# A mixture-of-experts layer in fp32: 64-column matmuls issued as pairs of 32-column matmuls in the first of two layers

## The chip, the cores and the metric

The kernel runs on one NeuronCore of one Trainium2 chip. The metric is the device time of one execution in microseconds (us), from its start to its end; lower is better. All arithmetic is fp32. TensorE's matrix multiply takes a stationary operand (here the token columns, loaded with LDWEIGHTS) and streams a moving operand (here the expert's weight rows) past it, up to 512 columns at a time, into PSUM. The number of stationary columns is the number of PSUM partitions that are written, and the partition at which the output starts says which columns of the array are used.

## What is computed

The program is two transformer blocks one behind the other, each of two layers. What matters here is the second block's feed-forward part, an expert-choice mixture of 16 experts. Layer 0 runs it on two token sets (512 latent tokens and 256 context tokens), layer 1 on the latent tokens only.

```python
def ec_moe(h, w_router, w_gate, w_up, w_down):
    bsz, n_tok, d = h.shape                       # d = 1024
    cap = EC_CAPACITY * n_tok // N_EXPERTS        # 64 of 512 latent tokens, 32 of 256 context tokens
    aff = jax.nn.softmax(jnp.einsum('bnd,de->bne', h, w_router).astype(jnp.float32), axis=-1)
    g, idx = lax.top_k(jnp.swapaxes(aff, 1, 2), cap)
    xs = jax.vmap(lambda hb, ib: hb[ib])(h, idx)
    hid = jax.nn.silu(jnp.einsum('becd,edf->becf', xs, w_gate)) * jnp.einsum('becd,edf->becf', xs, w_up)
    ye = jnp.einsum('becf,efd->becd', hid, w_down) * g[..., None].astype(h.dtype)
    return jax.vmap(lambda yb, ib: jnp.zeros((n_tok, d), h.dtype).at[ib.reshape(-1)].add(yb.reshape(-1, d)))(ye, idx)
```

Each expert has three weight matrices of 1024x1024 fp32 (4 MB each).

## The kernel before, in words

The program runs the first block, then for each layer of the second block a mixer (attention and convolution), a router, and the 16 experts (`pe_experts`, `experts_act`, `experts_dve`, `experts_pool`, one function per engine). Each engine's instructions stand in program order; engines meet through semaphores. The experts run as 8 rounds of two (`rounds`): the first round is written out, the other seven are a hardware loop.

**TensorE** does for each expert: the gate product, the up product, the turning (transposes) of the next expert's gathered rows (`turn_xs`, L1042), the transposes of the hidden rows (L1095, L1100), and the down product. Each product (`product`, L1048 to L1064) goes through 8 steps, one for each 128 rows of the weight matrix (`for k in range(KD)`), so an expert has 24 steps. A step waits for its weight slot (a 128x1024 piece, 512 KB), and then issues:

- two matmuls for the 64 latent tokens (L1055), one for each half of the 1024 weight columns. The stationary operand is 64 columns wide, the moving operand 512. Half 0 writes partitions 0 to 63 and half 1 partitions 64 to 127 of the same PSUM bank, `dst`.
- in layer 0 also four matmuls for the 32 context tokens (L1060), one for each quarter of the weight columns: 32 stationary columns, 256 moving ones, into partitions 0, 32, 64 and 96 of another bank, `dstc`.

The profile counts each fp32 matmul as two MATMUL and two LDWEIGHTS records, so a step of layer 0 has 4 and 8 of each, and one of layer 1 has 4.

**The weights** come through 24 slots (`expert_slot`: 12 of a ring, and 12 in buffers that are free by then, which the profile names mixT, mixcT, v, probs, qz and kz). SyncE issues the load of a slot for the next expert (L2369) as soon as the step that used it has signalled `moe_k`. So the loads run one expert ahead of the matmuls.

**GpSimd** gathers the token rows of a later expert (L1231; 96 rows of 4 KB in layer 0, 64 in layer 1) and adds the finished rows to the output in DRAM (L1272). **ScalarE and VectorE** apply the activation, copy products out of PSUM and scale the results.

After layer 0's experts the residual and norm of that layer run, then layer 1's mixer, router and experts.

Of the kernel before, what the change touches and what calls it, by code (L numbers as in the profile page):

```python
# [27 lines left out]
KD = D // P  # L28
# [21 lines left out]
CAP = 2 * SEQ // EXPERTS  # L50
# [80 lines left out]
def build_program(nc, a, known, banks, sem_names):  # L131
# [6 lines left out]
    with ExitStack() as ctx:  # L138
# [3 lines left out]
        def sem(name):  # L142
            if name not in sems:
                sems[name] = ctx.enter_context(nc.semaphore(name))
            return sems[name]

        def done(name, event=None, by=1):

            if not frozen[0]:
                counts[name] = counts.get(name, 0) + by  # L150
                marks[(name, event)] = counts[name]
            return sem(name), by

        def at(name, event=None):

            return sem(name), known.get((name, event), 1)

        def emptied(job):

            for name in ("evac_act", "evac_dve"):  # L160
                if (name, job) in known:
                    return at(name, job)
            return at("evac_act", job)
# [85 lines left out]
        ps = ctx.enter_context(nc.psum_tensor("ps", [P, 8, 512], F32))  # L249
# [744 lines left out]
        def at_round(name, event, i, back=0):  # L994

            per = known.get(("per_round", event[0], name), 1)
            return sem(name), i * per + max(known.get((name, event), 1) - back * per, -back * per + 1)
# [8 lines left out]
        def expert_slot(s):  # L1006
            return ring[:, s, :] if s < RING else spare[s - RING]

        def slot_count(s, l, u, i):

            return i * 32 + (banks.get(("moe_slot", l, s), 0) + 16 * (u + 1))

        def rounds(eng, l, body):

            before = dict(counts)
            body(0)
            per = {k: counts[k] - before.get(k, 0) for k in counts if counts[k] != before.get(k, 0)}
            frozen[0] = True
            with eng.Fori(1, ROUNDS) as i:
                body(i)  # L1020
            frozen[0] = False
            for k, n in per.items():
                marks[("per_round", l, k)] = n
                counts[k] = before.get(k, 0) + ROUNDS * n

        def settled(eng, count):


            return count if first_round(count) else eng.compute_val(count)

        def first_round(i):
            return isinstance(i, int)

        def pe_experts(pe, l):
            rows = CAP + (CAP_C if l == 0 else 0)
            G, U, GC, UC, Y, YC = 2, 3, 4, 5, 6, 7

            def turn_xs(i, u, event):

                for hb in range(2):  # L1040
                    for c in range(4):
                        mm = nc.tensor.transpose(ps[:, hb, c * 96:c * 96 + rows],  # L1042
                                                 xs[0:rows, (u + 1) % 2, (4 * hb + c) * P:(4 * hb + c + 1) * P],
                                                 ident[0:rows, 0:rows])
                    mm.then_inc(*done("xs_turned", (l, event, hb)))

            def product(i, u, m, lhs, dst, dstc, last_event):


                for k in range(KD):  # L1050
                    s = KD * m + k
                    pe.wait_ge(sem(f"slot{s}"), slot_count(s, l, u, i))
                    w = expert_slot(s)
                    for half in range(2):
                        mm = nc.tensor.matmul(ps[64 * half:64 * half + 64, dst, :], lhs[:, k, 0:CAP],  # L1055
                                              w[:, half * 512:(half + 1) * 512], start=(k == 0), stop=(k == KD - 1),
                                              skip_group_check=True)
                    if l == 0:
                        for q in range(4):
                            mm = nc.tensor.matmul(ps[32 * q:32 * q + 32, dstc, 0:256], lhs[:, k, CAP:CAP + CAP_C],  # L1060
                                                  w[:, q * 256:(q + 1) * 256], start=(k == 0), stop=(k == KD - 1),
                                                  skip_group_check=True)
                    mm.then_inc(*done("moe_k", (l, u, m, k)))


            pe.wait_ge(*emptied(("topT", l)))
            pe.wait_ge(*emptied(("grow", l, 1, 1 if l == 0 else 0, 1)))
            pe.wait_ge(sem("gathered0"), known.get(("gather", l, 0), 16))
            turn_xs(0, -1, "first")

            def body(i):
                for u in range(2):
                    b = u

                    if u == 0:
                        if first_round(i):
                            pe.wait_ge(*at("xsT_act", (l, "first")))
                            pe.wait_ge(*at("xsT_dve", (l, "first")))
                        else:
                            pe.wait_ge(*at_round("xsT_act", (l, 1), i, 1))  # L1080
                            pe.wait_ge(*at_round("xsT_dve", (l, 1), i, 1))
                    else:
                        pe.wait_ge(*at_round("xsT_act", (l, 0), i))
                        pe.wait_ge(*at_round("xsT_dve", (l, 0), i))
                    product(i, u, 0, xsT[:, b, :, :], G, GC, None)
                    product(i, u, 1, xsT[:, b, :, :], U, UC, None)

                    count = settled(pe, gather_count(l, u, i))
                    pe.wait_ge(*emptied(("topT", l)))
                    pe.wait_ge(sem(f"gathered{(u + 1) % 2}"), count)  # L1090
                    turn_xs(i, u, u)

                    pe.wait_ge(*at_round("hid", (l, u, 0), i))
                    for c in range(4):
                        mm = nc.tensor.transpose(ps[:, G, c * P:(c + 1) * P], hid[:, c * P:(c + 1) * P], ident)  # L1095
                    mm.then_inc(*done("hid_turned", (l, u, 0)))
                    if l == 0:
                        pe.wait_ge(*at_round("hid", (l, u, 1), i))
                        for c in range(2):
                            mm = nc.tensor.transpose(ps[:, GC, c * P:(c + 1) * P], hidc[:, c * P:(c + 1) * P], ident)  # L1100
                        mm.then_inc(*done("hid_turned", (l, u, 1)))
                    pe.wait_ge(*at_round("hidT", (l, u), i))

                    if not (first_round(i) and u == 0):
                        pe.wait_ge(*at_round("ye_copied", (l, 1 - u), i, 1 - u))
                    product(i, u, 2, hidT, Y, YC, None)

            rounds(pe, l, body)

        def gather_count(l, u, i):  # L1110

            return i * 16 + (known.get(("gather", l, 1 - u), 16) + 16 * u)
# [1322 lines left out]
```

## Time and profile before

| | us |
|---|---|
| median of 3 runs | 3107.52 |
| lowest and highest run | 3103.11, 3107.66 |
| span of the profiled execution, first to last instruction | 3105.2 |
| TensorE busy in it | 2721.4 (88%) |
| VectorE, ScalarE, GpSimd busy | 1024.7, 745.5, 254.5 |

For the profiled execution the page gives its span and no separate total; the three runs are other executions. Layer 0's experts lie between about 1423 and 2076 us of the span, layer 1's between about 2558 and 3066 us. In the rows of the trace a busy matmul has the time until its last result is out, so the times of neighbouring matmuls overlap; how fast a stream of them runs is read from the starts.

### The profile page before, as it was taken

The page shows a single profiled execution, that of the slowest core. Times are in us where ns is not written, and L with a number is a line of the kernel's source. Part 1 is how long each engine was busy: PE and PEld are TensorE (multiplying, and loading weights), DVE is VectorE, ACT ScalarE, POOL GpSimd, SP SyncE. Part 2 cuts the span into 40 slices and gives each one's busy share as a digit, 9 for nine tenths or more (in the row PEclk, how much of TensorE's full clock was granted, in tenths as well). Part 3 has the DMA queues.
Part 4 walks back from the last instruction along what each step waited for, and adds up shares of the span by engine and source line. Part 5 has one row for each costly group of instructions (what it writes and reads, how often), then busy time and mean ns, then how long its engine had stood idle before and what let it go on. Part 6 is the DMA issues. An engine that isn't in the chain of part 4 may idle for free. (4 is left out here: it accounts for less than half of the span.)

```text
span 3105.2 us, 44305 instructions
## 1 busy us (share of the span) xinstructions
PE 2721.4 (88%) x17378; PEld 1465.2 (47%) x17378; DVE 1024.7 (33%) x2278; ACT 745.5 (24%) x1857; POOL 254.5 (8%) x314
## 2 busy tenths in 40 slices
PE   7998999999989899987999999976899969788783
PEld 3664684665867666782222222213666753222221
DVE  3123430224347763553111111126752551011012
ACT  2233411343221453331111111113243321000000
POOL 1000100001000010021000000010000021001001
PEclk9999999999999999987999999997899979999997
DMA  7342614444331011047999999971002059999996
GB/s 217 106 125 67 182 36 114 124 114 120 106 82 34 1 27 48 31 160 278 334 327 330 329 332 331 324 213 39 26 8 75 28 202 387 389 397 396 390 397 233
DMA packets 354638, 579.26 MB, mean 187 GB/s; under 512 B 18592, under 2 KB 242048, under 8 KB 354496
## 3 DMA queue, kind: packets, MB, share of 16 engines
q1 hardware_dynamic: 339040, 523.47, 49.0%
q0 software_dynamic: 15312, 53.67, 6.2%
q8 instruction: 100, 1.64, 0.2%
q14 instruction: 42, 0.34, 0.0%
q10 hardware_dynamic: 144, 0.14, 0.0%
HBM read 554.12 MB, written 23.07 MB: 186 GB/s over the span
## 5 line engine op out<-in xcount | busy, mean ns | idle before, releaser
L441 PE MATMUL ps<-hT,ring 128*128 128x512 f32 x1088 | 482.3, 603 | 5.7 <-ACT hT L1403 4.3
L1055 PE MATMUL ps<-ring,hT 128*64 128x512 f32 x1536 | 424.8, 647 | 63.1 <-DMA ring<-in_w_gate 29.7
L441 PEld LDWEIGHTS ps<-hT,ring 128*128 128x128 f32 x1088 | 209.4, 194 | 264.5 <-issue 257.1
L687 PE MATMUL ps<-ring,mixT 128*128 128x128 f32 x2048 | 232.6, 276 | 0.8 <-DVE mixT L1539 0.8
L1055 PEld LDWEIGHTS ps<-ring,hT 128*64 128x64 f32 x1536 | 86.3, 141 | 308.6 <-DMA ring<-in_w_gate 121.3
L687 PEld LDWEIGHTS ps<-ring,mixT 128*128 128x128 f32 x2048 | 231.0, 193 | 1.3 <-DVE mixT L1539 1.3
L1190 DVE TENSOR_TENSOR work<-work,ps 128x512 f32<-128x512 f32 x32 | 22.0, 688 | 632.3 <-PE ps L1060 326.3
L487 PE MATMUL ps<-kz,qz 96*128 96x256 f32 (+3 forms) x384 | 156.9, 492 | 26.3 <-DVE qz L1965 10.7
L1212 DVE SCALAR_TENSOR_TENSOR hcT<-hcT,gates,work 64x1024 f32<-64x1024 f32 (+1 forms) x48 | 61.3, 1276 | 354.5 <-ACT hcT L1156 221.3
L1126 ACT ACTIVATE hT<-ps,modc 128x64 f32<-128x64 f32 x204 | 62.3, 403 | 400.3 <-PE ps L1042 400.3
L1580 ACT ACTIVATE probsT<-ps 128x512 f32<-128x512 f32 (+3 forms) x280 | 120.3, 455 | 140.2 <-PE ps L527 113.3
L1567 ACT ACTIVATE probs<-ps,col 128x256 f32<-128x256 f32 (+5 forms) x216 | 136.5, 632 | 70.9 <-DVE col L1517 37.0
L513 PE MATMUL ps<-const,probs 128*128 128x128 f32 x752 | 122.9, 280 | 20.5 <-DVE probs L1531 18.4
L1055 PE MATMUL ps<-mixT,hT 128*64 128x512 f32 x512 | 133.4, 612 | 7.0 <-DMA mixT<-in_w_up 6.9
L1513 DVE TENSOR_REDUCE col<-ps 128x1 f32<-128x256 f32 (+4 forms) x136 | 78.9, 580 | 178.1 <-PE ps L487 175.3
L1060 PE MATMUL ps<-ring,hT 128*32 128x256 f32 x1536 | 123.5, 393 | 0.0
L1272 POOL DMA_INDIRECT y_moe<-hcT,idx_to x32 | 46.3, 1447 | 918.2 <-DVE hcT L1212 891.8
L1152 ACT ACTIVATE hcT<-ps 64x512 f32<-64x512 f32 x64 | 37.9, 593 | 338.1 <-PE ps L1060 201.2
L1531 DVE TENSOR_SCALAR probs<-probs,col 128x256 f32<-128x256 f32 (+5 forms) x216 | 112.0, 519 | 7.6
L513 PEld LDWEIGHTS ps<-const,probs 128*128 128x128 f32 x752 | 89.9, 143 | 42.2 <-DVE probs L1531 30.9
L452 PE MATMUL ps<-ring,hT 128*128 128x128 f32 x896 | 103.0, 277 | 4.5 <-ACT hcT L1403 4.5
L452 PEld LDWEIGHTS ps<-ring,hT 128*128 128x128 f32 x896 | 102.8, 194 | 7.7 <-ACT hcT L1403 4.8
(275 smaller groups left out, 3386.3 us busy)
## 6 DMA issues: line engine op xcount, KB each, us to landing
ring<-in_w_gate SPq DMA_DIRECT2D x256, 512.0 KB, 8.9
ring<-in_w_up SPq DMA_DIRECT2D x128, 512.0 KB, 8.7
mixT<-in_w_up SPq DMA_DIRECT2D x128, 512.0 KB, 7.6
ring<-in_w_mod SPq DMA_DIRECT2D x96, 512.0 KB, 5.2
ring<-in_w_in SPq DMA_DIRECT2D x82, 512.0 KB, 7.3
mixcT<-in_w_down SPq DMA_DIRECT2D x64, 512.0 KB, 8.7
qz<-in_w_down SPq DMA_DIRECT2D x64, 512.0 KB, 11.8
kz<-in_w_down SPq DMA_DIRECT2D x64, 512.0 KB, 12.9
```

The source lines that it names most:

```text
L441: mm = nc.tensor.matmul(ps[:, b, 0:n], w[:, k, :], rhs[:, k, 0:n], start=(k == 0), stop=(k == KD - 1))
L452: mm = nc.tensor.matmul(ps[:, b, t * P:(t + 1) * P], lhs[:, k, t * P:(t + 1) * P], w[:, k, :], start=(k == 0), stop=(k == KD - 1))
L487: mm = nc.tensor.matmul(S[:, o:o + rhs.shape[-1]], lhs, rhs, start=lhs is not ident, stop=True, skip_group_check=True)
L513: mm = nc.tensor.transpose(ps[:, 4 + n % 2, i * P:(i + 1) * P], p_sbuf(u)[:, j * P:(j + 1) * P], ident)
L687: mm = nc.tensor.matmul(ps[:, b, c * P:(c + 1) * P], lhs[:, k, tl * P:(tl + 1) * P], ws[c][:, k, :], start=(k == 0), stop=(k == KD - 1))
L1055: mm = nc.tensor.matmul(ps[64 * half:64 * half + 64, dst, :], lhs[:, k, 0:CAP], w[:, half * 512:(half + 1) * 512], start=(k == 0), stop=(k ...
L1060: mm = nc.tensor.matmul(ps[32 * q:32 * q + 32, dstc, 0:256], lhs[:, k, CAP:CAP + CAP_C], w[:, q * 256:(q + 1) * 256], start=(k == 0), stop ...
L1126: ins = nc.scalar.activation(xsT[:, (u + 1) % 2, c, o:o + n], ps[:, 0, c * 96 + o:c * 96 + o + n], ACT.Identity, bias=sh, scale=sc)
L1513: nc.vector.tensor_reduce(nmax(u), s_psum(u), AX, ALU.max, negate=True).then_inc(*done("nmax", u))
L1531: nc.vector.tensor_scalar(p, p, rinv(u), None, ALU.mult).then_inc(*done("probs_normed", u))
L1567: nc.scalar.activation(p_sbuf(u), s_psum(u), ACT.Exp, bias=nmax(u), accum_out=rsum(u)).then_inc(*done("probs", u))
L1580: nc.scalar.activation(probsT[:, n % 2, blocks[0]:blocks[-1] + 1, :], ps[:, 4 + m % 2, 0:len(blocks) * P].rearrange("p (b q) -> p b q", q= ...
```

## The change

In `product`, where the layer is 0, the loop over halves has an inner loop over groups of 32 token columns. Each matmul of 64 stationary columns becomes two of 32 with the same moving operand, which write partitions `64*half` and `64*half + 32` of the same bank. In layer 1 the step of the inner loop is 64, so that the same matmul as before is issued there. The matmuls of the context tokens, the waits and the signals stay as they are.

```diff
@@ -1051,10 +1051,13 @@
                     s = KD * m + k
                     pe.wait_ge(sem(f"slot{s}"), slot_count(s, l, u, i))
                     w = expert_slot(s)
+                    step = 32 if l == 0 else CAP
                     for half in range(2):
-                        mm = nc.tensor.matmul(ps[64 * half:64 * half + 64, dst, :], lhs[:, k, 0:CAP],
-                                              w[:, half * 512:(half + 1) * 512], start=(k == 0), stop=(k == KD - 1),
-                                              skip_group_check=True)
+                        for g in range(0, CAP, step):
+                            o = 64 * half + g
+                            mm = nc.tensor.matmul(ps[o:o + step, dst, :], lhs[:, k, g:g + step],
+                                                  w[:, half * 512:(half + 1) * 512], start=(k == 0),
+                                                  stop=(k == KD - 1), skip_group_check=True)
                     if l == 0:
                         for q in range(4):
                             mm = nc.tensor.matmul(ps[32 * q:32 * q + 32, dstc, 0:256], lhs[:, k, CAP:CAP + CAP_C],
```

On TensorE, at the start of layer 0's experts, the instructions stand so (the shapes are stationary columns x moving columns; a row is a run of matmuls of one line; - is before, + is the change, whose lines stand 3 further down):

```order
-L1055 MATMUL ps<-ring,hT 64x512 x2
-L1060 MATMUL ps<-ring,hT 32x256 x4
...
+L1058 MATMUL ps<-ring,hT 32x512 x4
+L1063 MATMUL ps<-ring,hT 32x256 x4
```

Each pair of rows is one step. The order of the steps and of everything between them is the same; only the first run of each step has four matmuls in the place of two.

## Rows read from the trace of the kernel before

**Rows 1.** Layer 0's L1060 matmuls: records, duration ns min/median/max, first and last start.

```profile
L1060 PE MATMUL ps<-ring,hT x1536: 379/403/636, 1425.0 to 2053.6; 128*32 128x256 f32 x192
L1060 PE MATMUL ps<-mixT,hT x512: 379/391/403, 1445.7 to 2059.9; 128*32 128x256 f32 x171
```

**Rows 2.** Stretches of layer 0's experts and layer 1's: busy, PEclk, DMA share, GB/s.

```profile
1466.31:2075.88 609.57, 594.58 (x4534) 147.81 (x4530) 97.18 (x210) 89.06 (x241) 41.87 (x60) 1.00 0.94 321
2832.00:2864.00 32.00, 25.81 (x104) 6.63 (x104) 3.66 (x7) 3.07 (x7) 2.74 (x4) 0.95 1.03 393
```

**Rows 3.** Timeline of TensorE, layer 0: start us, us, engine line op [idle before].

```profile
1500.53 1.08 PE L1055 MATMUL ps<-qz,work 128*64 128x512 f32 x4
1501.54 0.64 PE L1060 MATMUL ps<-qz,work 128*32 128x256 f32 x8
...
1506.84 1.08 PE L1055 MATMUL ps<-ring,hT 128*64 128x512 f32 x4
```

**Rows 4.** Timeline of TensorE, layer 0, between up and down product.

```profile
1450.98 0.88 PE L1042 MATMUL ps<-const,hT 96*128 96x96 f32 x8
...
1453.69 1.08 PE L1055 MATMUL ps<-mixcT,work 128*64 128x512 f32 x4 [0.90 <-DVE work L1202]
...
2062.95 1.08 PE L1055 MATMUL ps<-mixcT,work 128*64 128x512 f32 x4 [0.90 <-DVE work L1202]
```

**Rows 5.** Timeline, one step of layer 0 in short windows: the records' later passes apart.

```profile
1466.32 1.08 PE L1055 MATMUL ps<-ring,hT 128*64 128x512 f32 x4
...
1466.80 0.60 PE L1055 MATMUL ps<-ring,hT 128*64 128x512 f32 x2
...
1467.32 0.42 PE L1060 MATMUL ps<-ring,hT 128*32 128x256 f32 x4
...
1467.56 0.40 PE L1060 MATMUL ps<-ring,hT 128*32 128x256 f32 x4
```

**Rows 6.** Timeline of TensorE, layer 1, steps of one shape whose weights had landed.

```profile
2825.88 1.06 PE L1055 MATMUL ps<-v,work 128*64 128x512 f32 x4
2826.74 1.06 PE L1055 MATMUL ps<-probs,work 128*64 128x512 f32 x4
2827.60 1.91 PE L1055 MATMUL ps<-qz,work 128*64 128x512 f32 x8
```

**Rows 7.** Timeline of TensorE, projections of the second block: shapes change, 128 stationary columns stay.

```profile
944.68 7.31 PE L452 MATMUL ps<-ring,hT 128*128 128x128 f32 x64
951.82 3.74 PE L452 MATMUL ps<-ring,hcT 128*128 128x128 f32 x32
955.39 7.07 PE L441 MATMUL ps<-hcT,ring 128*128 128x256 f32 x32
962.30 7.31 PE L452 MATMUL ps<-ring,hcT 128*128 128x128 f32 x64
...
985.08 13.90 PE L441 MATMUL ps<-hT,ring 128*128 128x512 f32 x32
998.81 1.46 PE L441 MATMUL ps<-hcT,ring 128*128 128x256 f32 x6
```

**Rows 8.** Timeline of TensorE, the modulation product: 32 stationary columns at four places.

```profile
138.24 1.96 PE L596 MATMUL ps<-ring,cond 128*32 128x128 f32 x64
140.12 0.49 PE L487 MATMUL ps<-kz,qz 96*128 96x128 f32 x2
```

**Rows 9.** Waits in layer 0's experts: total us, times, longest.

```profile
POOL y_moe L1272 <- DVE hcT L1212: 491.6, 15, 49.4
DVE work L1190 <- PE ps L1060: 298.1, 15, 20.0
```

**Rows 10.** Timeline of TensorE, layer 1: first wait for weights, later starts of down products.

```profile
2619.49 1.08 PE L1055 MATMUL ps<-mixT,hT 128*64 128x512 f32 x4 [1.29 <-DMA mixT<-in_w_up]
...
2657.91 1.94 PE L1055 MATMUL ps<-mixcT,work 128*64 128x512 f32 x8 [0.79 <-DVE work L1197]
...
2890.53 1.94 PE L1055 MATMUL ps<-mixcT,work 128*64 128x512 f32 x8 [0.97 <-DVE work L1197]
```

**Rows 11.** Start of both expert stages: first product of layer 1, first reload of layer 0.

```profile
1426.19 12.62 SPq L2369 DMA_DIRECT2D ring<-in_w_gate  x8
...
2557.74 12.59 PE L1055 MATMUL ps<-ring,hT 128*64 128x512 f32 x48 [1.24 <-ACT hT L1126]
```

## The prediction

> **What bounds the kernel now.** I read first which stage the change touches. Its matmuls are those of layer 0's experts, 16 experts of 24 steps, 384 steps. The list of one line's instructions for L1060, which exists in layer 0 only, puts them between 1425 and 2076 us [rows 1]. Then I read what each engine does there. From 1466.31 to 2075.88 us, 15 experts, TensorE is busy for 594.58 of 609.57 us at a granted clock of 1.00, that is 2.4 GHz; the DMA engines move 321 GB/s [rows 2]. In the list of waits of this stretch no matmul waits for a weight load; the others wait for TensorE: VectorE's first instruction of an expert waits up to 20.0 us for it, and GpSimd's scatter is behind that chain [rows 9]. So this stage lasts as long as TensorE's stream of steps, and every nanosecond of a step counts 384 times until something else becomes the bound.
>
> A step takes (1506.84 - 1500.53) / 4 = 1.5775 us, of which the two 64-column matmuls take 1.01 and the four 32-column ones 0.57 [rows 3]. Between the up and the down product there are 2.71 us of transposes and of waiting for hidden rows [rows 4]. 24 x 1.5775 + 2.71 = 40.57; measured from down product to down product over 15 experts it is (2062.95 - 1453.69) / 15 = 40.62. The model of a period holds to 0.05 us.
>
> **Where the 1.5775 us of a step go.** The short windows divide a step into its four passes: the 64-column group starts at 1466.32, its second pass at 1466.80, the 32-column group at 1467.32, its second pass at 1467.56 [rows 5], and the next step 1.5775 behind the first, at 1467.90. That makes passes of 0.48, 0.52, 0.24 and 0.34 us. What a pass costs when nothing changes between passes is read elsewhere. In layer 1, whose steps have only the 64-column pair, steps with landed weights start 0.86 us apart, 0.43 a pass [rows 6]. In the projections, with 128 stationary columns throughout, 32 records of 512 moving columns take 13.73 us, 0.429 each, and 32 of 256 take 6.91 us, 0.216 each [rows 7]. Four such passes are 2 x 0.429 + 2 x 0.216 = 1.290 us. A step of layer 0 takes 0.2875 us more: about 0.05 in its first pass, 0.09 in its second, 0.02 in the third, and 0.11 in the fourth.
>
> What is special about these steps is that the width of the stationary operand alternates, 64, 32, 64, 32. At each change there are two charges: the last pass before it is longer (0.09 and 0.11), as if the array had to run empty, and the first pass behind it is longer by about the time of a weight load that is not hidden (0.05 for 64 columns, 0.02 for 32). Where the width stays, neither is there: not in layer 1 [rows 6], and not in the projections, where both the moving length (128, 256, 512) and the bank change with no charge at the border [rows 7]. TensorEngine Tiling (Array Packing) of the Trainium skill, Key Properties, says that a change of tiling mode drains TensorE, but gives no price.
>
> **The change, part by part.**
>
> *Removed:* the change of width within a step and between steps of one product. All eight matmuls of a step are now 32 columns wide. By the sum above a step falls from 1.5775 to 1.290 us: 0.2875 x 384 = **110.4 us**. Bounds for this term: below, that some 5 ns per pass are added, the fixed part in [rows 7]: a pass is 0.1116 us for 128 columns (7.14 / 64) and 0.429 for 512, so 0.83 ns a column and 5 ns over; if the four-place passes had that twice, 0.27 a step, 103 us. Above, the full removal without any fixed cost, 0.297 a step, 114 us. I take 0.2875, since rows 7 are streams with the same lengths of pass.
>
> *Added:* two matmuls a step, that is four MATMUL and four LDWEIGHTS records more, 768 matmuls in all. If they ran behind the others, each step would double. They don't have to: the 32-column group of today starts four matmuls together, since all four records begin before the window at 1467.56 and 0.24 us later the next four start, where one alone streams 0.216 [rows 5]. The modulation product is the nearest row for a long stream of them: 64 records of 32 columns at four places, 128 moving columns, in 1.96 us with the following work at 140.12, 1.88 behind the start [rows 8]. That is 16 passes of at most 0.1175, against 0.1116 in [rows 7] with no tiling at all; the rest is the drain at its end. So four at once cost nothing over one, and issuing 8 records with their 8 loads per pass of 0.11 us keeps up. After the change there are 8 + 8 records per 0.43 or 0.22 us, a slower pace. I cost the added ones at nothing; the cover is the stream of moving columns, and if it were gone they would cost the rivals' prices below.
>
> *At the borders:* the first load behind the transposes is of 32 columns and not 64, 0.03 us less for two borders an expert, under 1 us in all, left out. The first two or three steps of the stage run below full clock and gain a little less or more; also left out.
>
> *What is late next.* The period becomes 24 x 1.290 + 2.71 + 0.05 = 33.7 us. ScalarE and VectorE need about 6 us each of it (89.06 and 97.18 in 15 experts [rows 2]); GpSimd's scatter has a wait of some 30 us to give [rows 9]. The weight loads are the candidate. Layer 1 is bound by them: there the DMA engines are at 1.03 and 393 GB/s [rows 2], and its period is (2890.53 - 2657.91) / 7 = 33.2 us [rows 10]. An expert of layer 0 moves the same 24 x 0.524 MB = 12.58 MB of weights, and 96 rows of 4 KB gathered and scattered in the place of 64: 13.37 MB against 13.11. The floor is 33.2 x 13.37 / 13.11 = 33.9 us, 0.2 more than TensorE needs. That does not yet stall it, since the loads are nearly an expert ahead. Layer 1 gives the lag: its loads can restart at about 2559 [rows 11]; the load that first makes TensorE wait is the 39th after that, due 39 x 33.2 / 24 = 54 us later, 2613; it is used at 2619.49 [rows 10], so about 7 us are to be added. In layer 0 the reloads start at 1426.19 [rows 11]; those for 15 experts are there by 1426 + 15 x 33.9 + 7 = 1942. TensorE's last step starts at 1423 + 16 x 33.7 + 1 = 1963. So the loads stay ahead to the end, by 21 us. I cost the loads at nothing in the stage and 1 us behind it, where the loads for layer 1's mixer now overlap the last scatter.
>
> **The sum.** 3105.2 - 110.4 + 1 = 2995.8 us of span. The median of the runs is 2.3 above the profiled span, so 2998 us.
>
> **Rivals.**
>
> *The loads become the bound* (chance 0.12). The DMA share, and not the bytes, may be the true measure: 0.94 at a period of 40.62 us; if 1.03 is the most, the floor is 40.62 x 0.94 / 1.03 = 37.1 us. The reloads would then end at 1426 + 15 x 37.1 + 7 = 1989.5, 26 us after the last step wants its slot. The gain is 84, the time 3024. For it: the share is already high. Against: layer 1 moves 393 GB/s through the same kind of loads [rows 2]. It decides from a floor of (1963 - 7 - 1426) / 15 = 35.3 us.
>
> *One weight load per pass is exposed* (0.05). With 32 columns the price is what the first pass has too much, 0.240 - 0.216 = 0.024 us; four passes, 0.096; the step is 1.386, the gain 73.5, the time 3034. Against it: no such gap in [rows 6] or [rows 8]. TensorE: Matmul & The Clock Gate of the Trainium skill, Part 3, says that a weight load overlaps a running matmul only if it is for another group of rows. All loads here are for all 128 rows, so by that rule they would be exposed, and the time would be this rival's or the next one's; the trace disagrees, at 0.43 us a pass in layer 1 where that rule wants 0.48.
>
> *Every weight load is exposed* (0.04), the other side. There are now 16 loads a step. If each held up the stream by 0.024 us, the step would be 1.290 + 0.384 = 1.674 us, 0.097 more than now: 37 us slower, 3145. It decides from 0.2875 / 16 = 18 ns a load. The place would be the four 512-column matmuls, of which pairs read the same weights; no row has just that. Against: 64 loads in 1.88 us [rows 8] leave 5 ns apiece over the streaming.
>
> *The width is not the cause* (0.05). If the 0.2875 us came from going back and forth between two banks and two lengths within one step, it would stay: 3107. Rows 7 change both without a charge, but every 8 records or more, not every two.
>
> **How the numbers follow.** The forecast has what is left, 0.74, and its own range is 2990 to 3004 (103 to 114 us gained, some us for the last loads and the runs' scatter of 4.6). With the first rival 0.86 are covered; the range so is 2990 to 3030. A difference of 0.2% (6 us) is about what a measurement of this kernel can tell from none. Faster: 0.74 + 0.12 + 0.05 = 0.91. Same: 0.05. Slower: 0.04.
>
> **What would show it.** In the profile of the changed kernel: steps of layer 0 that start 1.29 us apart, with four records at the start of each pass (1.39: exposed loads; 1.58: the width wasn't it); 24 of them and an unchanged 2.7 us between products, periods of 33.7; no matmul of layer 0 waiting for a weight load, with a DMA rate near 390 GB/s; layer 1 unchanged at periods of 33.2 and everything from the end of layer 0's experts on about 110 us earlier. Waits for the loads late in the stage with steps of 1.29 would be the first rival; a time within 6 us of before, or above it, would show the forecast wrong.

## The result, and the profile after

The changed kernel takes 3003.31 us (median of 4 runs, 2999.04 to 3020.04) against 3107.01 (median of 4 runs), a ratio of 0.9678 with a 95% interval from 0.9652 to 0.9704. The forecast was 2998, with a range from 2990 to 3030. The profiled execution took 3002.31 us, its span is 3000.5.

The timeline of TensorE in the stretch that [rows 3] show, in the changed kernel:

```profile
1505.00 1.04 PE L1058 MATMUL ps<-ring,hT 128*32 128x512 f32 x8
1505.86 0.61 PE L1063 MATMUL ps<-ring,hT 128*32 128x256 f32 x8
1506.29 1.04 PE L1058 MATMUL ps<-ring,hT 128*32 128x512 f32 x8
1507.15 0.61 PE L1063 MATMUL ps<-ring,hT 128*32 128x256 f32 x8
1507.58 0.61 PE L1058 MATMUL ps<-ring,hT 128*32 128x512 f32 x4
```

A step starts every 1.29 us where it was 1.5775. The 512-column group has twice the records and takes 0.86 us where it took 1.01, and the 256-column group, whose instructions are unchanged, takes 0.43 where it took 0.57. The second number points most plainly at what the change removes: nothing was done to L1063, yet it is faster beside neighbours of its own width. That the width of the neighbours decides this is tested in experiment 4.

The busy times by stretch, as in [rows 2] (busy of PE, PEld, DVE, ACT and POOL, then clock, DMA share, GB/s):

```profile
1600.00:1700.00 100.00, 97.03 (x1182) 40.46 (x1178) 19.43 (x42) 17.75 (x48) 8.36 (x12) 1.00 1.03 387
1800.00:1900.00 100.00, 97.03 (x1182) 40.53 (x1178) 19.43 (x42) 17.75 (x48) 8.35 (x12) 1.00 1.03 392
```

The DMA engines now run at the share and nearly the rate that they have in layer 1, and TensorE is still busy for 97% of the time. The list of waits of TensorE and its load queue in this stage names VectorE's hidden rows, and no weights. It also has a line that was not there before (who waited on whom: total us, times, longest):

```profile
PE ps L1058 <- DVE work L1205: 13.4, 15, 0.9
...
PE ps L1058 <- issue: 5.4, 1, 5.4
```

"issue" is a wait for nothing that the profile shows. The timeline has its place, between the fourth and the fifth expert:

```profile
1560.65 0.61 PE L1063 MATMUL ps<-kz,work 128*32 128x256 f32 x8
1566.67 1.94 PE L1058 MATMUL ps<-ring,hT 128*32 128x512 f32 x8 [5.41 <-issue]
1568.37 1.09 PE L1063 MATMUL ps<-ring,hT 128*32 128x256 f32 x8
1569.23 1.94 PE L1058 MATMUL ps<-ring,hT 128*32 128x512 f32 x8
1570.93 0.67 PE L1063 MATMUL ps<-ring,hT 128*32 128x256 f32 x8
```

This is the first jump back of TensorE's loop over rounds. Behind the pause one whole step runs with starts 2.56 us apart, twice the usual, at a granted clock of 0.50 in the window from 1565 to 1570 us: after the standstill the array is at its lower level, 1.2 GHz. That expert's period is 41.62 us; the other 14 are 33.75 to 33.85.

The starts of the down product give the account of the stage; they answer to [rows 4]:

```profile
1446.05 0.62 PE L1063 MATMUL ps<-mixT,hT 128*32 128x256 f32 x8
1446.60 0.88 PE L1042 MATMUL ps<-const,hT 96*128 96x96 f32 x8
...
1449.30 1.07 PE L1058 MATMUL ps<-mixcT,work 128*32 128x512 f32 x8 [0.90 <-DVE work L1205]
...
1964.60 1.07 PE L1058 MATMUL ps<-mixcT,work 128*32 128x512 f32 x8 [0.90 <-DVE work L1205]
```

From the first down product to the last it is 515.30 us where it was 609.26. The two ends of the stage are its first step and the first transpose of the next stage (L644). Before:

```profile
1423.14 1.98 PE L1055 MATMUL ps<-ring,hT 128*64 128x512 f32 x4 [2.12 <-ACT hT L1126]
...
2098.78 1.54 PE L644 MATMUL ps<-const,kz 128*128 128x128 f32 x6 [23.14 <-DVE kz L1304]
```

After:

```profile
1424.04 1.93 PE L1058 MATMUL ps<-ring,hT 128*32 128x512 f32 x8 [2.12 <-ACT hT L1129]
...
1998.33 1.97 PE L644 MATMUL ps<-const,kz 128*128 128x128 f32 x8 [23.20 <-DVE kz L1307]
```

So the stage lasts 574.3 us where it lasted 675.6, 101.4 less: 5.3 are gained up to the first down product, 94.0 between the first and the last, and 2.1 behind the last. The spans differ by 104.7. The rest lies in stretches whose instructions the change leaves alone: the stage starts 0.9 us later, and from L644 to the end of the span it is 1002.2 us where it was 1006.4. In the profiles of the experiments the stretch from L644 on takes between 1003.3 and 1006.2, and the stage starts between 1422.1 and 1427.9, so differences of some us there say nothing about the change.

### The profile page after: what moved, and what is told of

Read it like the earlier page. It is cut to its first block and busy times, and to the rows that moved or that the text cites. A ratio compares the mean times of both kernels' runs of the same rounds, so it can differ in the third digit from the quotient of the medians.

```text
span 3000.5 us, 47377 instructions
## 1 busy us (share of the span) xinstructions
PE 2611.7 (87%) x18914; PEld 1525.0 (51%) x18914; DVE 1022.8 (34%) x2278; ACT 744.5 (25%) x1857; POOL 255.1 (9%) x314
## 5 line engine op out<-in xcount | busy, mean ns | idle before, releaser
L1058 PE MATMUL ps<-ring,hT 128*32 128x512 f32 (+1 forms) x2304 | 417.9, 624 | 66.5 <-DMA ring<-in_w_gate 29.6
L1058 PEld LDWEIGHTS ps<-ring,hT 128*32 128x32 f32 (+1 forms) x2304 | 98.6, 123 | 265.3 <-DMA ring<-in_w_gate 121.3
L1058 PE MATMUL ps<-mixT,hT 128*32 128x512 f32 (+1 forms) x768 | 132.8, 598 | 8.2 <-DMA mixT<-in_w_up 8.1
L1063 PE MATMUL ps<-ring,hT 128*32 128x256 f32 x1536 | 119.0, 382 | 0.0
L1063 PEld LDWEIGHTS ps<-ring,hT 128*32 128x32 f32 x1536 | 50.4, 111 | 117.3 <-issue 117.3
```

The source lines that it names most:

```text
L1058: mm = nc.tensor.matmul(ps[o:o + step, dst, :], lhs[:, k, g:g + step], w[:, half * 512:(half + 1) * 512], start=(k == 0), stop=(k == KD - ...
```

## Experiments

**1. The change once more.** The pause was not foreseen, so it is first asked whether it comes again.

> The changed kernel once more. In its profile one period of layer 0's experts was 41.6 us where the 14 others were 33.8: TensorE stood still 5.4 us with no releaser at the first step behind the first jump back of the loop, and then ran two steps at the lower clock. Theory A (instruction fetch: the body has a third more TensorE instructions, and behind the jump they must come over DMA queues that are full of weight loads): a pause of some us at a border of rounds in this profile too, not always the same border, and times that scatter upward from about 2995. Theory B (a chance event of that one execution): 15 periods of 33.8 us, and a profiled time near 2995.

3001.42 us (6 runs, 2994.01 to 3021.42). The pause is there again, at the same border:

```profile
PE ps L1058 <- DVE work L1205: 11.7, 13, 0.9
PE ps L1058 <- issue: 5.4, 1, 5.4
```

The fifth expert's period is 41.56 us, the others 33.74 to 33.85. So theory B, by which it was a chance event of one execution, falls. Of theory A the pause at a border of rounds and the scatter of the times are borne out; its cause, a fetch through full queues, is asked in experiment 6. Two of these six runs and one of the first four took about 3020 us, as much above 2995 as three such pauses would cost; none of these three was profiled.

**2. The same matmuls as before, with half as many changes of width.** It keeps the instructions and the shapes of before and halves the changes of width, so it tells these changes from the number and the shape of the matmuls.

```diff
-                for k in range(KD):
-                    (wait for the slot; latent, 64 wide; context, 32 wide)
+                group = 2 if l == 0 else 1
+                for k0 in range(0, KD, group):
+                    for k in range(k0, k0 + group):
+                        (wait for the slot; latent, 64 wide)
+                    for k in range(k0, k0 + group):
+                        (context, 32 wide)
```

> Same matmuls as before, 64 columns wide for the latent tokens, but in layer 0 two steps' 64-wide pairs come first and then both steps' 32-wide ones: the width changes half as often, the number of instructions is that of before. Theory (each change of width is charged): two steps take 2 x 1.290 + 0.2875 = 2.87 us in the place of 3.155, the gain is 0.144 x 384 = 55 us, 3052. Rival (the 64-wide matmuls or the two banks of a step are the cost, and 32-wide ones are faster by themselves): 3.155 us for two steps, 3107.

3049.39 us (5 runs), a ratio of 0.9818 (0.9805 to 0.9831): 57 us gained with the instructions of before, where 55 were expected. Its timeline, in which two steps are one pair of rows, or two where the weights' names differ:

```profile
1603.44 1.08 PE L1052 MATMUL ps<-v,work 128*64 128x512 f32 x4
1604.35 1.03 PE L1052 MATMUL ps<-probs,work 128*64 128x512 f32 x4
1605.30 0.64 PE L1059 MATMUL ps<-v,work 128*32 128x256 f32 x8
1605.76 0.61 PE L1059 MATMUL ps<-probs,work 128*32 128x256 f32 x8
1606.31 1.94 PE L1052 MATMUL ps<-qz,work 128*64 128x512 f32 x8
```

Two steps take 2.87 us. The first 64-wide group takes 0.91 (it pays for entering) and the second 0.95 (it pays for leaving); the two 32-wide groups take 0.46 and 0.55. Without a change of width the 64-wide group takes 0.86 [rows 6] and the 32-wide one of 256 columns 0.43 (in the change). So 64-wide matmuls are not slow in themselves. Experiment 2 doesn't separate the width from the bank and the moving length, since it halves their changes too. The changed kernel does: it still goes from one bank and one length to the other twice in every step, and has lost the whole charge.

**3. The same number of instructions, with the widths of before.** The latent matmuls are cut along the moving side instead.

```diff
-                    for half in range(2):
-                        (64 stationary columns, 512 moving)
+                    n = 256 if l == 0 else 512
+                    for c in range(0, 512, n):
+                        for half in range(2):
+                            (64 stationary columns, n moving, bank columns c to c + n)
```

> The kernel before, with each 64-wide matmul of layer 0 cut along the moving side: four of 64 stationary and 256 moving columns in the place of two of 512. The number of TensorE instructions is exactly that of the change, the widths alternate as before. Theory (the gain is from the widths, added instructions cost nothing): steps of 1.58 to 1.59 us, periods near 40.7, 3107 to 3112. Rival (more and smaller instructions are what helped): steps near 1.29, 3000. On the pause: A2 (length of the body) expects one of some us behind the first jump back here too, A1 (full queues) none or a shorter one, since the loads need 34 of 40.7 us.

3115.39 us (10 runs), a ratio of 1.003 (1.0017 to 1.0042). More matmuls do not help: steps are 1.58 us apart as before, and they are so although all matmuls of a step now have one moving length, 256.

```profile
1602.16 1.08 PE L1057 MATMUL ps<-ring,hT 128*64 128x256 f32 x8
1603.17 0.64 PE L1062 MATMUL ps<-ring,hT 128*32 128x256 f32 x8
1603.74 1.08 PE L1057 MATMUL ps<-ring,hT 128*64 128x256 f32 x8
```

Periods are 40.74 against 40.62, so the 768 added matmuls cost about 2 us. The time is 3 us above the expected range, and the reason is a pause here too, at another border (before the ninth expert, where the period is 47.46), though the loads run at 323 GB/s:

```profile
1756.20 1.98 PE L1057 MATMUL ps<-ring,hT 128*64 128x256 f32 x8 [5.25 <-issue]
```

So the pause belongs to the added instructions, not to the shorter step or the new width.

**4. The change in gate and up only.** It asks both for the price per step and for the length at which the pause comes.

```diff
-                    step = 32 if l == 0 else CAP
+                    step = 32 if l == 0 and m < 2 else CAP
```

> The change for the gate and up products only; the down product of layer 0 has its 64-wide matmuls back. Theory of the widths: steps of 1.290 us in gate and up and 1.5775 in down, periods of 16 x 1.290 + 8 x 1.5775 + 2.76 = 36.0 us, a gain of 256 x 0.2875 = 73.6 us, 3033. On the pause: a round has 1408 matmul and load records here, between 1152 (no pause in three profiles) and 1536 (a pause in each of five). If the length decides, either none or a pause like the others at a border of rounds; in the trace its sign is that instruction fetches stop for good after the second round or start again later.

3033.26 us (5 runs), a ratio of 0.9762 (0.9748 to 0.9775), against 3033 expected; periods are 36.01. The two kinds of step stand one behind the other in its timeline:

```profile
1603.64 0.64 PE L1063 MATMUL ps<-kz,work 128*32 128x256 f32 x8
1604.20 1.08 PE L1058 MATMUL ps<-kz,work 128*64 128x512 f32 x4
1605.21 0.64 PE L1063 MATMUL ps<-kz,work 128*32 128x256 f32 x8
1605.67 1.04 PE L1058 MATMUL ps<-ring,hT 128*32 128x512 f32 x8
1606.53 0.61 PE L1063 MATMUL ps<-ring,hT 128*32 128x256 f32 x8
1606.96 1.04 PE L1058 MATMUL ps<-ring,hT 128*32 128x512 f32 x8
```

The unchanged group of L1063 takes 0.56 us when a 64-wide group follows, 0.46 between a 64-wide group and a 32-wide one, and 0.43 with 32-wide ones on both sides. There is no pause.

**5. The floor of the loads in layer 0.** The prediction had two values for it, 33.9 by the bytes and 37.1 by the DMA share, and its largest rival hung on the second.

```diff
-                    if l == 0:
+                    if l == 0 and k == 0:
                         for q in range(4):
-                            (start=(k == 0), stop=(k == KD - 1))
+                            (start=True, stop=True)
```

> The kernel before, but the context tokens' products are computed from the first 128 weight rows only (their four matmuls in the first step of each product, none in the other seven): TensorE then needs about 25 us an expert, and the loads set the pace. It measures the floor of layer 0's loads with 96 rows gathered and scattered. By the bytes: later periods of 33.9 us, the last step about 1942 to 1945, total about 2975. By the share of busy DMA time: periods of 37.1, the last step near 1989, total about 3022.

2983.3 us (4 runs), a ratio of 0.9604 (0.959 to 0.9618). Two starts of the hidden transposes (L1095), 11 experts apart, give the floor:

```profile
1563.56 0.66 PE L1095 MATMUL ps<-const,work 128*128 128x128 f32 x4
...
1938.62 0.66 PE L1095 MATMUL ps<-const,work 128*128 128x128 f32 x4
```

(1938.62 - 1563.56) / 11 = 34.1 us. The value from the bytes was right to 0.2 us; the last step starts at about 1947, which the expectation put at 1942 to 1945. The total is 8 us above the 2975 expected: some 3 of them are the later last step, another 4 the wait before the next layer's first transpose (27.4 us in the place of 23.1), and the rest was not followed up. The share of 0.94 in [rows 2] did not mean that 9% was all there was left: the stage could be loaded in 34.1 / 40.6, 84% of its time.

**6. The pause: half of each load, and no loop.** If the pause is a fetch that has to queue behind weights, half of the bytes should shorten it. If it is a fetch behind a jump, it should go away without the jump.

```diff
-                                sp_.dma_start(expert_slot(s), src).then_inc(sem(f"slot{s}"), 16)
+                                n = 512 if l == 0 and not (first_round(i) and u == 0) else 1024
+                                sp_.dma_start(expert_slot(s)[:, 0:n], src[:, 0:n]).then_inc(sem(f"slot{s}"), 16)
```

> The changed kernel, but in layer 0 from the second expert on only the first 512 of the 1024 columns of each weight slot are loaded (the rest keeps old values, so the experts' results are not those of the reference); TensorE's instructions and waits are the change's. The DMA engines carry about half of the bytes in that stage. Theory A1 (the pause behind the first jump back comes from fetching through full DMA queues): no pause or one of under 1 us, 15 periods of 33.84. Theory A2 (it comes from the length of the body, whatever the queues carry): the pause of 5.4 us stays and the period at that place is 41.6 us.

3002.63 us (4 runs, 2997.84 to 3011.97), ratio 0.9667 (0.9645 to 0.9688). At 207 GB/s in the stage the pause is still there, at the same border, a little shorter, and the period is 40.85:

```profile
1563.22 1.93 PE L1058 MATMUL ps<-ring,hT 128*32 128x512 f32 x8 [4.07 <-issue]
```

The result lies between the two theories: A1 wanted the pause gone or under 1 us, A2 unchanged at 5.4. Half of the bytes took 1.3 us off the 5.4, so the traffic may have a part in the length of the pause, but not the larger one. Pauses at full traffic measured 5.4, 5.4, 6.3 and 5.5 us, and one profile of the halved loads is all there is.

```diff
-            with eng.Fori(1, ROUNDS) as i:
-                body(i)
+            if written_out:                     # TensorE, layer 0
+                for i in range(1, ROUNDS):
+                    body(i)
+            else:
+                with eng.Fori(1, ROUNDS) as i:
+                    body(i)
```

> The changed kernel, with TensorE's eight rounds of layer 0 written out one behind the other in the place of a loop: no jump back on TensorE in that stage. Theory A (the pause is the fetch behind a jump): no pause, 15 periods of 33.84 us, span near 2993, about 8 less than the profiled execution of the change, and less scatter. Rival (instructions are late under full DMA queues wherever they stand): pauses remain, at other places, and the time is no better than 3003.

2996.92 us (5 runs, 2993.2 to 2999.35), ratio 0.9645 (0.9633 to 0.9658). All 15 periods are 33.75 to 33.85, and "issue" is gone from TensorE's waits. The runs scatter over 6 us, those of the looped version over 21 (2999 to 3020) and 27 (2994 to 3021). The span is 2995.1 us, 5.4 under that of the change where 8 were expected: the 15 periods together are 7.7 shorter, as they should be, but the stretch from L644 to the end is 3.1 longer.

> The written-out version once more, as the neighbour of the early start: 2997, periods of 33.84, no pause, a wait of 23 us for layer 1's first norm.

2997.89 us (5 runs, 2996.47 to 3003.06), no pause, the wait before the next layer's first transpose 23.3 us. The interval of the ratio of the written-out version (0.9633 to 0.9658) overlaps that of the change (0.9652 to 0.9704). So the times alone don't show that it is faster; what is shown is that the pause is gone from the stage in both profiles.

Instructions reach the engines over a DMA queue of their own, and the list of queues by window shows when (queue: packets, MB, share). Before, the first window from 1440 to 1580 us has

```profile
q8 instruction: 8, 0.13, 0.4%
```

and that from 1670 to 2040 has no such line. The change, from 1440 to 1559 and from 1559 to 1577, the window of the pause:

```profile
q8 instruction: 11, 0.18, 0.6%
...
q8 instruction: 4, 0.07, 1.7%
```

From 1577 to 1645 it has 5 more, and from 1645 to 1960 none. The version that is written out, from 1645 to 1960:

```profile
q8 instruction: 29, 0.48, 0.6%
```

The reading: a loop body is fetched in pieces of 16 KB as it is first run through, and afterwards kept, as nothing is fetched in the later rounds. In the kernel before, the first jump back finds its target there. In the change, with 1536 matmul and load records a round in the place of 1152, it does not, four pieces come at the time of the pause, and the body is fetched again. Written out, the same instructions come all the time, every 11 us, and nothing waits, since no jump breaks the order. The 29 pieces in 315 us are 6.2 for each round of 67.7 us, by which the body of the changed kernel is about 102 KB (an estimate). Runtime: NRT & Kernel Launch of the Trainium skill, Instruction fetch mechanics, says that fetching ahead is sequential and that a taken jump whose target isn't held stalls the engine; the trace agrees on the stall. On what is held the same section gives TensorE 128 KiB, and also speaks of a window of two pieces of 16 KiB. By the window one would expect a stall at every jump, by the 128 KiB none; the traces show six jumps in the stage with none (before), or with one or two that pause (1536 records a round).

**7. Both layers.**

```diff
-                    step = 32 if l == 0 else CAP
+                    step = 32
```

> The change, with 32-wide matmuls in layer 1 as well, where nothing else is 32 wide and the loads are the bound. Theory: layer 1's steps with landed weights stay 0.86 us apart, its later periods 33.2, and the time is the change's, 3002 within 6 us. On the pause: layer 1's body grows from 8 to 16 records a step, its queues are as full, so if it comes with the length, one may appear behind layer 1's first jump back; there the loads are the bound and it would be hidden or cost a little. Rival (a 32-wide stream pays per load): layer 1's first periods rise above 23.05 us.

3005.29 us (4 runs), ratio 0.9657 (0.9638 to 0.9677). Layer 1 is as it was. Its first down products (at 16 records for two steps):

```profile
2482.17 1.92 PE L1058 MATMUL ps<-mixcT,work 128*32 128x512 f32 x16 [0.78 <-DVE work L1200]
...
2505.22 1.92 PE L1058 MATMUL ps<-mixcT,work 128*32 128x512 f32 x16 [0.79 <-DVE work L1200]
```

23.05 us apart, as with 64 columns: where the width does not change, 32 wide and 64 wide cost the same, and twice the loads are hidden. In layer 0 this profile has two pauses (periods of 42.52 and 42.34), the second with 9 more instruction packets from 1825 to 1915. Layer 1's loop has none.

**8. A version beyond the change.** Between up and down product TensorE waits 0.90 us for two copies by VectorE. The down product's latent matmuls need only the first. This version also has TensorE's rounds of layer 0 written out.

```diff
-                    ins = nc.vector.tensor_copy(dst, src)
+                    nc.vector.tensor_copy(dst, src).then_inc(*done("hidT", (l, u, 0)))
...
-                        ins = nc.vector.tensor_copy(dst, src)
-                    ins.then_inc(*done("hidT", (l, u)))
+                        nc.vector.tensor_copy(dst, src).then_inc(*done("hidT", (l, u, 1)))
...
+                    if l == 0 and m == 2 and k == 0:
+                        pe.wait_ge(*at_round("hidT", (l, u, 1), i))
```

> The version with TensorE's rounds written out, in which the down product's first latent matmuls start when VectorE has copied the latent hidden columns, and only the context matmuls wait for the second copy (0.41 us). Theory: that copy leaves the path, the period falls from 33.84 to about 33.4, 16 times 0.4 is 6.5 us: about 2990. The floor of the loads measured 34.1 a period; the deficit of 15 times 0.7 is less than the lead of some 17 us, so no matmul waits for a load. Rival (the loads bind first): waits for weights at the end of the stage, and no gain over 2997.

2995.62 us (5 runs), ratio 0.9636 (0.9621 to 0.9651), where 2990 was expected.

> The early start of the down product with rounds written out, once more, now beside the written-out version in the same job. Its periods measured 33.51 against 33.84, 5 us over 15 experts, but the medians differed by 1.3 only (2995.6 and 2996.9, from different jobs). Theory: the 5 us are real in the stage, and the times differ by about 5 when taken side by side. Rival: what the stage gives is lost behind it, where layer 1 waits for the last scatter and reloads (TensorE's wait there was 25.9 us in place of 23).

2999.14 us (5 runs), ratio 0.9648 (0.9635 to 0.9662), beside 2997.89 for its neighbour. In the stage the theory holds: the wait falls from 0.90 to 0.56, and the periods are 33.51 instead of 33.84 in both profiles; no matmul waits for a load. But the total is not measurably better. A part of the 5 us is visibly given back: GpSimd waits longer for the last scatter to land, and with it everything behind. Before, and in the second profile of this version:

```profile
2087.97 2.24 POOL L2301 DMA_DIRECT2D h<-y_moe  x4 [4.55 <-DMA y_moe<-hcT,idx_to]
```

```profile
1981.14 2.23 POOL L2312 DMA_DIRECT2D h<-y_moe  x4 [6.47 <-DMA y_moe<-hcT,idx_to]
```

TensorE's wait before the next layer's first transpose is 25.9 and 25.2 us in the two profiles of this version, and 22.9 and 23.3 in those of its neighbour: some 2 us of the 5. That the last scatter now lands among the reloads of the ring for layer 1's mixer is a possible cause; this was not tried. From its first step to L644 the stage is still shorter, 565.0 and 564.2 us against 567.3 and 567.7, but the stretch ahead of it varies by more: it ends at 1427.9, 1427.9 and 1427.4 in three of these profiles and at 1422.5 in the fourth. So the gain of some 3 us is lost in the scatter of the runs. The version is no better than the written-out one by any measurement made here.

## Why the prediction was right

*What bounds the stage.* Right: TensorE's stream did, before and after. The added DMA rate came out at 387 to 392 GB/s against "near 390", and no matmul of layer 0 waits for weights.

*The term of the step*, 0.2875 us x 384 = 110.4 us. Right: 1.290 was forecast and 1.29 measured. The cause was argued from [rows 5] to [rows 7]. It is now shown by three measurements together: experiment 2 has the old instructions and half the changes of width (57 us gained, 55 expected), experiment 3 has the new number of instructions, one moving length and the old widths (no gain), and the changed kernel itself still changes bank and length twice a step without a charge. One reading of the prediction here is off by a factor: [rows 8] have four MATMUL records with four loads a pass, not eight with eight, and the change's passes have four and four too, so the comparison holds.

*The added matmuls at nothing.* Right for their execution: 1.29 us a step leaves no room for them, and layer 1's 23.05 us stay with twice the records. Wrong by omission for what it takes to bring them there. The step that failed is the sentence on what is "Added": it asked whether issuing keeps up, in the stream of the modulation product, and not how long the loop body becomes. The pause costs 7.8 us in the profiled execution, 5.4 of standstill and the rest in steps at the lower clock, and it makes the changed kernel's runs scatter. Experiments 3, 4 and 6 put it on the length of the body behind a jump. How the length does it is read from the instruction packets and was not tested further.

*The borders, left out as under 1 us.* Mis-sized and with the wrong sign. The period fell by 6.78 us, from 40.62 to 33.84, and not by 24 x 0.2875 = 6.90: of the fourth pass's extra 0.11 us, one in 24 stays, since behind the up product TensorE still goes over to the wider transposes (1446.05 to 1446.60 is 0.55 us where such a group takes 0.43 inside). That is 0.12 x 16 = 1.9 us lost. The first steps of the stage, also left out, gave 0.8 us more: up to the first down product 5.3 us are gained where 16 steps less one border make 4.5. The granted clock is low there for two steps, before and after.

*The sum for the stage:* 110.4 - 1.9 + 0.8 - 7.8 = 101.5 us, against 101.4 measured from the first step to L644.

*The 1 us behind the stage*, for the last loads: not there. TensorE's wait before L644 is 23.20 us where it was 23.14.

*The whole:* 109.4 us of span were forecast and 104.7 measured. The stage gave 9.0 less than its 110.4, the term of 1 us was not needed, the stage began 0.9 late, and the stretch behind it came out 4.2 shorter. That last part is luck: nothing in the prediction speaks of it, and no profile of the experiments shows that stretch as long as before or as short as after the change. Without it the time would have missed the forecast by about 9 us, and still have been inside the range.

*The rivals.* The loads do not bind: their floor is 34.1 us. It is above TensorE's 33.84, as the prediction said, and the lead of nearly one expert carries the 16 experts through. Exposed weight loads, once or each time, are excluded by the 1.29 us. (Its argument against the second, that 64 loads leave 5 ns apiece over the streaming, is misread: 1.88 us less 16 passes of 0.1067, the bare 0.83 ns a column, leave 0.17 us, 2.7 ns a load. It was far from the 18 ns that decide in either case.) That the bank and the length are the cause and not the width is excluded by the changed kernel, which keeps their changes, and by experiment 3. TensorE: Matmul & The Clock Gate of the Trainium skill, Part 3, says that a weight load overlaps a running matmul only where it is for another group of rows. This is not borne out here: a step of 1.29 us leaves no room for loads that are not hidden, though all of them are for the same 128 rows.

## What to carry to other kernels

When small matmuls of different stationary widths alternate, read the time from start to start of each pass, and look for the same shapes in a stream where the width stays: here each change of width cost about 0.14 us, 0.29 for a pair, and it was worth either cutting the wider one or doing the same width for two steps at a time (half the gain, no added instruction, no pause). Before adding instructions to a hardware loop count the length of its body, and after it look for an "issue" wait at the jump and at the instruction queue's packets by window. A high share of busy DMA time does not say how much more could be moved; the bytes against the rate of a stage that is bound by them did.

## What the runs showed of the hardware beyond what was expected

- A loop body of 1152 matmul and load records a round ran without a pause in two profiles and one of 1408 in the one profile there is; one of 1536 had a pause in five of five profiles, four times at the first jump back, once at the third, and in one of them at the fifth as well. The pause lasts 4.1 to 6.3 us, and its whole cost is 6.7 to 8.7 us with the steps at 1.2 GHz behind it. Why only one or two of the six jumps pause is open; the first lies where the body is still being fetched, the later ones come after a long stretch without any fetch.
- Four 32-wide matmuls of 512 columns, in pairs on the same moving data, stream in 0.43 us a pass, like two of 64 or one of 128.
